# A decoder layer with expert retrieval on one core: the output stage of three pairs of tiles shares its weight loads

## What is computed

```python
xn = rms_norm(x, attn_norm)
proj = xn @ w_in                              # q, k, v and the RWKV columns
o_da = attend(q, k, v, lam)                   # differential attention, causal, 4 heads
o_rw, wkv, shift = rwkv_time_mix(...)         # a recurrence over the rows, 8 heads
mixed = concatenate([o_da, o_rw])             # (rows, 1024)
h = x + mixed @ w_out                         # w_out: 1024 x 1024
hn = rms_norm(h, ffn_norm)
q = hn @ wq                                   # 8 heads, 2 maps of 128
s = einsum(q, sub_keys)                       # 2048 scores a row
# per row and head: the 16 best of each map, the 16 best of 256 sums: 128 experts a row
act = gelu(einsum('thkd,td->thk', u_tab[eidx], hn))
y = einsum('thk,thkd->td', gate * act, v_tab[eidx])
h = h + y ; y_out = rms_norm(h, final_norm)
```

## Time and profile before

| | |
|---|---|
| three runs | 3975.95, 3982.27 (median), 3983.49 us |
| profiled execution | 3977.58 us, its span 3975.8 us |
| DVE busy in the span | 2600.8 us (65%) |
| PE busy in the span | 2853.9 us (72%) |
| DMA | 1431.66 MB, mean 360 GB/s |
| first gather issued | 747.7 us after the span's start |

### The profile page before, as it was taken

The page is one execution under the profiler, slowest core; times in us unless marked ns, Lnnn a source line. Parts: engine busy times, 40 slices in busy tenths (PEclk is TensorE's granted clock), DMA queues, the critical chain, the costliest instruction groups (busy, mean ns, idle before and its releaser), DMA issues.

```text
span 3975.8 us, 54677 instructions
## 1 busy us (share of the span) xinstructions
PE 2853.9 (72%) x20366; PEld 1358.9 (34%) x20366; DVE 2600.8 (65%) x5836; ACT 1284.4 (32%) x3597; POOL 1358.7 (34%) x1190
## 2 busy tenths in 40 slices
PE   6899999675667576766766766677566758867564
PEld 3654454342224232322332243224222415521111
DVE  2423455488668848884987598658866776445954
ACT  1311211324333424342434334433433234422222
POOL 1000000243344434443434343434333456534443
PEclk9999999877877787788778777788787666777655
DMA  9535414899999999999999999999999999999998
GB/s 311 196 141 182 175 67 165 330 400 397 420 416 394 409 421 407 416 402 419 411 404 387 417 409 409 388 417 406 387 409 392 352 375 411 381 399 420 407 405 350
DMA packets 254682, 1431.66 MB, mean 360 GB/s; under 512 B 27376, under 2 KB 45312, under 8 KB 110160
## 3 DMA queue, kind: packets, MB, share of 16 engines
q0 software_dynamic: 163232, 1162.26, 72.1%
q1 hardware_dynamic: 91184, 265.89, 17.7%
HBM read 1373.21 MB, written 54.85 MB: 359 GB/s over the span
## 4 chain that ended last, share of the span: by engine, by line
PE 38%; DMA 32%; DVE 21%; issue 4%; ACT 2%; POOL 2%; SPq 0%; DVEq 0%; ACTq 0%; POOLq 0%
DMA pe_buf<-in_experts,pe_idx 28%; PE ip_B L1027 9%; DVE pe_buf L2262 7%; PE pe_psO L1413 5%; PE pe_B L1361 4%; PE pe_psH L1395 3%; PE pe_B L1344 3%; DMA op_wkr<-scratch_wk_rows 2%; PE pe_B L1061 1%; PE pe_B L1212 1%; DMA ip_w<-in_w_in 1%; POOL pe_buf L994 1%; DVE pe_top L2032 1%; DMA op_w<-in_w_out 1%; PE pe_B L1253 1%
## 5 line engine op out<-in xcount | busy, mean ns | idle before, releaser
L994 POOL DMA_INDIRECT pe_buf<-in_experts,pe_idx x1088 | 1277.3, 1174 | 2500.6 <-PE pe_psO L1413 1702.5
L2262 DVE CUSTOM_DVE_ANT_0 pe_buf<-pe_buf,pe_hnR 128x1024 f32<-128x1024 f32 x1088 | 1319.2, 1224 | 781.6 <-DMA pe_buf<-in_experts,pe_idx 768.5
L1413 PE MATMUL pe_psO<-pe_buf,pe_Z 128*32 128x256 f32 x8704 | 830.1, 485 | 547.2 <-ACT pe_Z L1690 510.4
L1413 PEld LDWEIGHTS pe_psO<-pe_buf,pe_Z 128*32 128x32 f32 x8704 | 222.9, 124 | 1187.3 <-ACT pe_Z L1690 888.3
L1684 ACT ACTIVATE pe_gelu<-pe_dot 128x1 f32<-128x1 f32 x1088 | 217.3, 200 | 1273.1 <-DVE pe_dot L2262 1270.3
L1395 PE MATMUL pe_psH<-pe_hn,pe_pick 128*128 128x512 f32 x544 | 402.9, 831 | 63.9 <-ACT pe_hnR L1666 61.6
L1027 PE MATMUL ip_B<-ip_w,ip_xT 128*128 128x512 f32 (+1 forms) x1008 | 433.3, 580 | 16.6 <-DMA ip_w<-in_w_in 16.6
L1690 ACT ACTIVATE pe_Z<-pe_gl,pe_gelu 128x8 f32<-128x8 f32 x1088 | 327.2, 301 | 43.0 <-ACT pe_gelu L1684 0.4
L1361 PE MATMUL pe_B<-op_wkr,pe_mix 128*128 128x512 f32 (+1 forms) x576 | 264.9, 604 | 9.2 <-DMA op_wkr<-scratch_wk_rows 9.2
L1027 PEld LDWEIGHTS ip_B<-ip_w,ip_xT 128*128 128x128 f32 x1008 | 190.8, 195 | 213.5 <-issue 208.1
L1666 ACT ACTIVATE pe_hnR<-pe_psH 128x512 f32<-128x512 f32 x272 | 159.0, 584 | 49.5 <-PE pe_psH L1395 48.8
(11 more groups left out here) (344 smaller groups left out, 3616.5 us busy)
## 6 DMA issues: line engine op xcount, KB each, us to landing
op_wkr<-scratch_wk_rows SPq DMA_DIRECT2D x36, 2048.0 KB, 11.8
ip_w<-in_w_in SPq DMA_DIRECT2D x18, 2048.0 KB, 9.1
op_w<-in_w_out SPq DMA_DIRECT2D x18, 2048.0 KB, 19.8
pe_buf<-in_experts,pe_idx POOLq DMA_INDIRECT x1088, 13.8
ip_w<-in_peer_wq SPq DMA_DIRECT2D x4, 2048.0 KB, 11.1
scratch_wk_rows<-wk_wkc SPq DMA_DIRECT2D x16, 512.0 KB, 6.2
tm_p<-scratch_kept_rows SPq DMA_DIRECT2D x8, 896.0 KB
tm_ps<-scratch_moved_rows SPq DMA_DIRECT2D x8, 896.0 KB
```

The lines of the kernel that those rows point to most:

```text
L994: pool.indirect_dma_start(buf[b][:], None, T["experts"], bass.IndirectOffsetOnAxis(ap=idx[:, t % 2, h * NJ + j:h * NJ + j + 1], axis=0)).t ...
L1413: last = nc.tensor.matmul(psO[32 * x:32 * x + 32, j // 4, :], Z[:, n % NZ, 24 - 8 * turn:56 - 8 * turn], buf[n % NBUF][:, D + x * QUART:D ...
L2262: nc.vector.tensor_tensor_reduce(buf[b][:, 0:D], buf[b][:, 0:D], hnR[:, n // PH % 2, :], 1.0, 0.0, ALU.mult, ALU.add, dot[:, n % (NBUF):n ...
```

## The change

Tiles 2 and 3, 4 and 5, 6 and 7 are pairs. The first tile of a pair goes through time mixing and attention, and its mixed rows are stored to DRAM (`keep_mixed`). The second follows. Then `project_pair` does the output stage of both: `w_out` and each piece of `wk_rows` are loaded once and used for both tiles. The first tile's scores go to `scores`; those of the second are stored to DRAM through a small stage and loaded into `scores` at slot 118 of the first tile's choice (`load_scores`). The front is now spread over groups: the first pair over slots 0 to 189, the next two over 256 slots each, the sample tile over 258. The choice of a pair's first tile (in gather tiles 1, 3 and 5) runs in slots 64 to 120 in place of 2 to 119, and in slots 62 to 123 of these gather tiles the front goes at 0.55 of its rate. In slots this gives:

| | before | now |
|---|---|---|
| gather tile 0 | tm, at, op of tile 2 | tm, at, keep of 2; tm of 3 |
| gather tile 1 | tm, at, op of tile 3 | at of 3 to slot 11; pair at slots 12 to 56; from 63 tm of 4 |
| gather tile 2 | tm, at, op of tile 4 | tm of 4 to slot 15; at, keep of 4; tm of 5; from 103 at of 5 |
| gather tile 3 | tm, at, op of tile 5 | pair at slots 2 to 55; from 63 tm of 6 |

Gather tiles 4 and 5 are as 2 and 3, with tiles 6, 7 and 8. In the diff the new stage is shown on SP (all DMAs), PE and DVE; ACT's part copies what PE has turned or summed, and takes the two roots of the norms.

```diff
-DURING = tuple((("tm", t + 2), ("at", t + 2), ("op", t + 2)) for t in range(LAST - 1))
-COST = {"gap": 3.0, "tm": 1.9, "at": 1.3, "op": 2.2, "topk": 1.8}
+PAIRS = ((2, 3), (4, 5), (6, 7))
+FIRSTS, SECONDS = tuple(a for a, _ in PAIRS), tuple(b for _, b in PAIRS)
+GROUPS = ((0,), (1,)) + PAIRS + ((LAST,),)
+PAIR_BY, PAIR_REST, REST_RATE = 62, 124, 0.55
+DURING = tuple((("tm", a), ("at", a), ("keep", a), ("gap", 5), ("tm", b), ("at", b), ("pair", a), ("gap", 4)) for a, b in PAIRS)
+DURING += ((("tm", LAST), ("at", LAST), ("op", LAST)),)
+COST = {"gap": 3.0, "tm": 1.9, "at": 1.3, "op": 2.2, "topk": 1.8, "keep": 1.0, "pair": 2.2}
 COST_LAST_AT = 3.3
...
+KEEP_STEPS, PAIR_STEPS = 2, 54
+SCORES_AT = {(0, 0): (31, 32), (0, 1): (33, 35), (1, 0): (37, 38), (1, 1): (39, 40), (0, 2): (43, 44), (1, 2): (45, 46),
+             (0, 3): (47, 48), (1, 3): (49, 50)}
+SCORES = tuple(sorted(SCORES_AT, key=lambda unit: SCORES_AT[unit]))
 TOPK_STEPS = 8 * PH // 2 + 6
-TOPK_FROM, TOPK_FROM_LAST, TOPK_TO = 2, 66, 120
+TOPK_FROM, TOPK_FROM_FIRST, TOPK_FROM_LAST, TOPK_TO = 2, 64, 66, 121
...
+def rate(n):
+
+    t, k = n // PER, n % PER
+    return REST_RATE if t + 1 in FIRSTS and PAIR_BY <= k < PAIR_REST else 1.0
+
 def pulls():
 
 
-    plan = []
-    for t, items in enumerate(DURING):
+    plan, start = [], 0
+    for group, items in enumerate(DURING):
         costs = costs_of(items)
+        end = (PAIRS[group][0] - 1) * PER + PAIR_BY if group < len(PAIRS) else (LAST - 1) * PER + LAST_OP_BY
         total, spent, i = sum(costs), 0.0, 0
-        length = PER if t < len(DURING) - 1 else PER + LAST_OP_BY
-        for k in range(length):
-            n = 0
-            while i < len(costs) and spent + costs[i] <= total * min(1.0, (k + 1) / (length - 2)) + 1e-6:
+        weight, passed = sum(rate(n) for n in range(start, end - 1)), 0.0
+        for slot in range(start, end):
+            n, passed = 0, passed + rate(slot)
+            while i < len(costs) and spent + costs[i] <= total * min(1.0, passed / weight) + 1e-6:
                 spent, i, n = spent + costs[i], i + 1, n + 1
             plan.append(n)
         if i != len(costs):
             raise ValueError("steps are left over")
+        start = end
...
-        first = TOPK_FROM if t < LAST - 1 else TOPK_FROM_LAST
+        first = TOPK_FROM_FIRST if t + 1 in FIRSTS else TOPK_FROM if t < LAST - 1 else TOPK_FROM_LAST
...
+        pr_mixed, pr_gf, pr_hnT1 = pr[1], mix, mix[:].rearrange("p (k t) -> p k t", k=KD)
+        pr_mT0 = pr_hnT0 = pr[3][:].rearrange("p (k t) -> p k t", k=KD)
+        pr_mT1 = pr[2][:].rearrange("p (k t) -> p k t", k=KD)
+        pr_stage = pr[2][:].rearrange("p (i n) -> p i n", i=2)
...
+            def load_wk(c_):
+                sp.dma_start(wkr[:, c_ % 2].rearrange("p c k n -> p c (k n)"), wk_rows[c_]).then_inc(wk_in[c_ % 2], 16)
+            def keep_mixed(t):
+                for k in range(KEEP_STEPS):
+                    if k == 0:
+                        sp.wait_ge(at["o_ready"], t + 1)
+                        sp.dma_start(T["mixed"][rows(t), :], mix[:]).then_inc(pair["mixed_stored"], 16)
+                    if k == 1:
+                        load_p(t + 1)
+                    yield
+            def store_scores(t, n_):
+                i = FIRSTS.index(t)
+                sp.wait_ge(op["sc_copied"], NC * t + SCORES.index((1, n_)) + 1)
+                if i and n_ == 0:
+                    sp.wait_ge(pair["scores_in"], 16 * i)
+                sp.dma_start(scores_rows[:, n_ * CW:(n_ + 1) * CW], pr_stage[:, n_ % 2]).then_inc(pair["scores_stored"], 16)
+            def load_scores(t):
+                i = FIRSTS.index(t)
+                sp.wait_ge(c["sc_read"], PH * (t + 1))
+                sp.wait_ge(pair["scores_stored"], 16 * NC * (i + 1))
+                sp.dma_start(scores[:].rearrange("p h n -> p (h n)"), scores_rows).then_inc(pair["scores_in"], 16)
+            def project_pair(t):
+                u, i = t + 1, FIRSTS.index(t)
+                for k in range(PAIR_STEPS):
+                    if k == 0:
+                        sp.wait_ge(at["o_ready"], u + 1)
+                        sp.wait_ge(pair["mixed_stored"], 16 * (i + 1))
+                        sp.dma_start(pr_mixed[:], T["mixed"][rows(t), :]).then_inc(pair["mixed_in"], 16)
+                        sp.dma_start(pr_h0[:], T["x"][rows(t), :]).then_inc(op["h_in"], 16)
+                    if k == 9:
+                        sp.wait_ge(op["turned"], 2 * u + 2)
+                        sp.dma_start(pr_gf[:], T["ffn_norm"].partition_broadcast(P)).then_inc(op["gf_in"], 16)
+                    if k == 19:
+                        sp.wait_ge(op["added"], t + 1)
+                        sp.dma_start(T["h"][rows(t), :], pr_h0[:]).then_inc(op["h_stored"], 16)
+                    if k == 21:
+                        sp.wait_ge(op["hn_ready"], t + 1)
+                        sp.dma_start(hn_rows[rows(t), :], pr_hn0[:]).then_inc(op["hn_stored"], 16)
+                    if k == 26:
+                        sp.wait_ge(op["summed"], 2 * u + 2)
+                        sp.dma_start(pr_h1[:], T["x"][rows(u), :]).then_inc(op["h_in"], 16)
+                        load_wk(0)
+                        load_wk(1)
+                    if k == 31:
+                        sp.wait_ge(op["added"], u + 1)
+                        sp.wait_ge(op["h_stored"], 16 * (t + 1))
+                        sp.dma_start(T["h"][rows(u), :], pr_h1[:]).then_inc(op["h_stored"], 16)
+                    if k == 33:
+                        sp.wait_ge(op["hn_ready"], u + 1)
+                        sp.wait_ge(op["hn_stored"], 16 * (t + 1))
+                        sp.dma_start(hn_rows[rows(u), :], pr_hn1[:]).then_inc(op["hn_stored"], 16)
+                    for n_ in range(NC):
+                        if n_ + 2 < NC and k == SCORES_AT[1, n_][1]:
+                            sp.wait_ge(op["scores_done"], NC * t + SCORES.index((1, n_)) + 1)
+                            load_wk(n_ + 2)
+                        if k == SCORES_AT[1, n_][1] + 2:
+                            store_scores(t, n_)
...
+                    yield
...
+                if t + 1 in FIRSTS and k == 118:
+                    load_scores(t + 1)
...
+            def project_pair(t):
+                u, i, group = t + 1, FIRSTS.index(t), group_of(t)
+                for k in range(PAIR_STEPS):
+                    if k in (6, 8):
+                        src, bank = ((pr_mixed, 0), (mix, 2))[(k - 6) // 2]
+                        if k == 6:
+                            pe.wait_ge(at["o_ready"], u + 1)
+                            pe.wait_ge(pair["mixed_in"], 16 * (i + 1))
+                        for n in range(KD):
...
+                    if 10 <= k < 26:
+                        second, half, n0 = (k - 10) // 8, (k - 10) // 4 % 2, (k - 10) % 4 * 2
+                        mT = (pr_mT0, pr_mT1)[second]
+                        if half == 0 and n0 == 0:
+                            pe.wait_ge(op["copied"], 2 * (t + second) + 2)
+                        if second == 0 and half == 0 and n0 in (0, 4):
+                            pe.wait_ge(w_out_in[n0 // 4], 16 * (group + 1))
+                        for n in (n0, n0 + 1):
+                            last = nc.tensor.matmul(B[:, 2 * second + half, :], mT[:, n, :], w_out[:, n, half * 512:(half + 1) * 512],
+                                                    start=(n == 0), stop=(n == KD - 1))
+                        if n0 == 6:
+                            last.then_inc(op["summed"], 1)
+                    if k in (22, 34):
+                        second, src, bank = ((0, pr_hn0, 0), (1, pr_hn1, 2))[(k - 22) // 12]
+                        pe.wait_ge(op["hn_ready"], t + second + 1)
+                        for n in range(KD):
+                            last = nc.tensor.transpose(B[:, bank + n // 4, n % 4 * P:(n % 4 + 1) * P], src[:, n * P:(n + 1) * P],
+                                                       ident[:])
+                            if n % 4 == 3:
+                                last.then_inc(op["hn_turned"], 1)
+                    for (second, n_), steps in SCORES_AT.items():
+                        if k in steps:
+                            q_, hnT = steps.index(k), (pr_hnT0, pr_hnT1)[second]
+                            if q_ == 0:
+                                pe.wait_ge(op["hnT"], 2 * (t + second) + 2)
+                                pe.wait_ge(wk_in[n_ % 2], 16 * (2 * group + n_ // 2 + 1))
+                                if n_ >= 2:
+                                    pe.wait_ge(op["sc_copied"], NC * t + SCORES.index((second, n_ - 2)) + 1)
+                            for n in range(4 * q_, 4 * q_ + 4):
+                                last = nc.tensor.matmul(B[:, 2 * second + n_ % 2, :], hnT[:, n, :], wkr[:, n_ % 2, :, n, :],
+                                                        start=(n == 0), stop=(n == KD - 1))
+                            if q_ == 1:
```

(29 more changed lines are left out.)

136 lines of the change are left out of this document (111 added, 25 removed).

## The result

The changed kernel takes 4048.88 us, the median of four runs (4042.54 to 4053.61), against 3979.11 us (3975.65 to 3983.49) of the kernel before on the same chip: ratio 1.016, 95% interval 1.014 to 1.018. The prediction of 3930, range 3902 to 3968, has the sign wrong.

What follows compares the result with a forecast made beforehand. DMA bytes were taken to bound the gather part, with DVE becoming the bound in the squeezed choice. From 3977.6 us, -72 + 18 - 5 + 8 + 3 = -48 gave 3929.6, stated as 3930, range 3902 to 3968.

Steps and rivals of the forecast that it cites:

- The first pair in 190 slots: Gather tile 0: denser front, DVE at 89%, time mixing's recurrence twice; +8 us (0 to +22).
- Bytes, -72: Output stages: each of three pairs saves net 9.96 MB, 23.9 us at 416 GB/s; -72 us if DMA stays full.
- Squeezed choice, +18: Slots 64 to 111 of gather tiles 1, 3, 5: DVE becomes the bound, filled to 92%; +18 us (0 to +60).
- Old dips, -5: Gather tiles 1, 3, 5: attention and choice no longer meet, so DMA dips mostly go; -5 us (0 to -11).
- Loads and waits of the pair stage, +3: Pair stage: late load of the second tile's `x` mostly regained, PE's work fits; +3 us (0 to +12).
- Tile's border, 0: End of the choice, a slot later at 120: POOL still gets its indices for slot 128 in time; 0 us.
- the slower rival: Borders after gather tiles 1, 3, 5: indices come late and DMA stands; 3990 to 4002 us, chance 0.06.
- Sample tile, 0: Sample tile gets 258 slots, not 192; its dip comes earlier, hardly flatter; 0 us (-8 to +5).
- DVE badly filled: Rival: squeezed stretches cost 16 to 20 us each, first pair 10 to 20; 3948 to 3970 us, chance 0.23.

Runs made afterwards that it cites:

- single pairs: Changed kernel with only tiles 2 and 3 paired, only 6 and 7, or only 4, 5 and 6, 7 as two pairs: 4034.7, 4073.2, 4060.3 us.
- denser front: Kernel before with an output step weighed 3.4 in place of 2.2, so time mixing and attention go at 2.26 units a slot, not 1.93: 4035.6 us.
- the two shifted plans: Kernel before with windows divided by length less one, not two; with the choice also ending at slot 121, not 120, 4032.2 us, without that 4020.9 us.
- lighter DVE: Choice without the steps turning places into expert numbers: 3984.2 us in the changed kernel, 3957.9 us in the kernel before.
- evened front: Changed kernel with the front at full rate beside the choice (REST_RATE 1.0, not 0.55): 4034.2 us; with the number-making steps of the choice also cut, 3971.6 us.
- runs with bytes alone: Changed kernel plus six 2 MB copies per pair stage: 4112.8 us; kernel before loading a quarter of output-stage weights for tiles 3, 5, 7: 3924.2 us.
- shorter stage: Changed kernel with a step of the pair stage weighed 1.5 in place of 2.2, so the stage gets fewer slots: 4071.2 us.
- window rounding alone: Kernel before with the front's windows divided by length less one in place of less two, the choice as before: 4020.9 us.

## Why the prediction was wrong

The step that failed is "The first pair in 190 slots", with the silent zero beside it for the crowded gather tiles 2 and 4. It reads "I take +8 (0 to +22)"; measured, gather tile 0 has 42 us of unused time more, and tiles 2 and 4 have 30 and 35, which had no term at all. I had judged these tiles by DVE's busy share, 89% of the need, from a sum of durations. The share came out as I had it (306 us worked, 307 worked out), but the share was not what bound them.

The runs showed two things in its place. The first is the recurrence at a low clock. Its loss is read from the traces; that the clock is its only reason is not shown. In gather tile 0 of the changed kernel, where the earlier trace rows had it losing 7 us:

```profile
845.50:855.50 10.00, 5.58 (x37) 3.34 (x32) 9.64 (x31) 1.33 (x5) 2.81 (x3) 0.56 0.96 363
855.50:865.50 10.00, 10.00 (x64) 5.59 (x56) 1.07 (x2) 3.03 (x11) 2.81 (x3) 0.50 0.68 238
865.50:875.50 10.00, 8.63 (x74) 5.96 (x72) 4.87 (x16) 0.00 (x0) 0.94 (x1) 0.50 0.54 206
875.50:885.50 10.00, 9.25 (x74) 4.94 (x72) 6.31 (x17) 3.42 (x12) 2.81 (x3) 0.73 0.36 134
```

By the table the recurrences account for 29 of the 140 us: in gather tiles 0, 2 and 4, where all six recurrences now stand, they lose 44 where three lost 9, and the other three lost 7 in tiles 1, 3 and 5. I had seen the row at 0.57 in the earlier trace rows and priced its second coming at its first price, with no question about what sets the clock there.

The second is the crowd of steps: the other 72 of the 107 us in gather tiles 0, 2 and 4, spread over time mixing and attention. Before, 107 of their steps stood in each tile beside some 36 slots of output stage; now 190, 167 and 167 stand there, and no such slots. The single pairs show that the loss goes with this crowd wherever it stands. An example, attention in gather tile 4, with PE's and DVE's waits for each other:

```profile
2407.80:2437.80 30.00, 19.71 (x136) 10.47 (x136) 24.92 (x62) 15.31 (x35) 10.59 (x10) 0.79 0.70 265
```

```profile
POOL pe_buf L1116 <- PE pe_psO L1588: 22.8, 7, 9.4
...
PE pe_B L1369 <- DVE at_prob L2265: 14.3, 2, 7.6
ACT pe_mix L1743 <- PE pe_B L1376: 6.0, 2, 3.4
```

No engine is full here, PE at 66% and DVE at 83%, and DMA stands at 0.70: each waits for another in turn, and the sums of the gathers stand behind. The denser front in the kernel before (+58) speaks for packing, but it shifted every step as well, and a shift alone cost 46 to 55. Outside the recurrences the two differ: the denser front left 68 us unused beyond before, of which 26 lie in the recurrences (16 to 42, with clocks of 0.65 to 0.82) and 42 elsewhere; the two shifted plans left only 11 and 12 more elsewhere. That the slots of the output stage had let the ring catch up is argued, not shown. How the 72 us divide between DVE's load, the order and the clock outside the recurrences is not settled: the lighter DVE left tiles 0, 2 and 4 nearly as they were, and the evened front helped 2 and 4 but moved the cost.

Point by point, the other terms:

- *Bytes, -72.* The size is right to 0.1 MB; the runs with bytes alone gave 70 to 85% of their DMA time, so by an estimate from these shares 11 to 22 of the 72 us may have been hidden under other work. Right in the main.
- *Squeezed choice, +18.* +25 alone; in the changed kernel 30 us more are unused in its slots, of the 40 more in gather tiles 1, 3 and 5. Right in kind, DVE being the bound there, and too small: the filling was 83 to 89% and not 92%. Inside its 0 to +60.
- *Old dips, -5.* Not seen: attention of tiles 5 and 7, at the end of gather tiles 2 and 4, left dips of its own (a DMA share of 0.65 from 1885 to 1905 us, 0.80 from 2650 to 2690). Within the 40 and 72 above.
- *Loads and waits of the pair stage, +3.* 13 us unused in slots 0 to 61 of gather tiles 1, 3 and 5, and 13 before. Right, and with no room to spare, as the shorter stage showed.
- *Tile's border, 0.* POOL's longest wait for a freed buffer is 17.8 us, and the view of its waits has no row for `pe_idx`. Right, so the slower rival did not happen.
- *Sample tile, 0.* Gather tiles 6 and 7 take 18 us less, some 12 of them bytes; inside the -8 to +5.
- *DVE badly filled*, the rival at 3948 to 3970, was nearest in kind. It had "the first pair 10 to 20" and nothing for the tiles behind. Its own sum, -3, gives 3975 us, which lies above the 3970 that it states.

The range was too narrow because it bounded each place that I had named, and no term stood for the plan as a whole: that the kernel before might owe time to where its steps fall. One row could have raised the question, the six recurrences of the kernel before at clocks between 0.68 and 0.89, with 9 and 0 us lost.

## What to carry to other kernels

In a kernel whose engines run one fixed order, a new plan is a cost of its own: before costing what a change removes, try the old work in a plan shifted by one slot; here that alone moved 1.2 to 1.4%. Work that shares a memory-bound stretch is hidden by its bytes, so taking bytes away from the one stage in which other engines rest gives less than it seems, and if their other work then crowds together, it can give less than nothing. And of a chain that leans on TensorE, look at the granted clock all through it: how long it stays low once TensorE is busy again was 7 us in one place and 31 in another of the same kernel.

## What the runs showed of the hardware

- TensorE's granted clock fell to 0.50 where PE had stood still for 3 to 4 us (kernel before) or 7.5 us (window rounding alone) ahead of a recurrence. It then stayed there for 7 us in gather tile 2 of the kernel before, for 31 us in its gather tile 0, and for 9 or 30 us in the shifted plan, with PE busy all the while. The Trainium skill (TensorE: Matmul & The Clock Gate, section HAM oscillation — how this bites in real kernels) has the first half, that a wait ahead of matmuls makes the next burst start at the lower level; these rows agree. That a busy PE is then released (section What's actually happening) fits the stretches of 7 and 9 us, but the 30 us do not bear it out. What kept it low was not found.
- A DMA share near 1 does not say that the rate is full. Gather tile 2 of the changed kernel has 0.96 at 379 GB/s, and the earlier trace rows 1.01 at 416: a loss of 5% in share and 9% in rate. The mean of a gather's 8 KB packet went from 318 to 335 ns in gather tile 0. The share counts a slower packet as busy, and so hides part of the idle time. That packets are slower because fewer gathers wait is my reading, not tested.
